# Two more product pairs before the recurrence, their first sums by DMA, and a root taken on GpSimd, in one layer of a streaming encoder

## Time and profile before

| | us |
|---|---|
| median of three runs | 1911.4 (1910.64 to 1913.37) |
| the profiled execution | 1911.61 |
| its span | 1909.8 |
| TensorE busy | 1889.0 (99%) |
| VectorE busy | 1355.4 (71%) |
| ScalarE busy | 859.4 (45%) |
| GpSimd busy | 84.7 (4%) |

### The profile page before, as it was taken

The page is one execution under the profiler, slowest core; times in us unless marked ns, Lnnn a source line. Parts: engine busy times, 40 slices in busy tenths (PEclk is TensorE's granted clock), DMA queues, the critical chain, the costliest instruction groups (busy, mean ns, idle before and its releaser), DMA issues.

```text
span 1909.8 us, 33091 instructions
## 1 busy us (share of the span) xinstructions
PE 1889.0 (99%) x13241; PEld 1864.5 (98%) x13241; DVE 1355.4 (71%) x2078; ACT 859.4 (45%) x1609; POOL 84.7 (4%) x136
## 2 busy tenths in 40 slices
PE   9999999999999999999999999999999999999997
PEld 8999999999999998999999999999999999999997
DVE  7798999899997754773444378976777776736363
ACT  5454444445434455551122355644454444635342
POOL 0010001000111111100000000000000000000000
PEclk9999999999999999999999999999999999999999
DMA  3445555455454754658131322221222223556654
GB/s 134 136 119 129 137 146 139 117 161 169 119 154 117 205 171 124 160 168 331 45 138 45 119 88 102 82 80 68 91 74 75 70 89 108 187 202 208 211 172 153
DMA packets 117031, 255.09 MB, mean 134 GB/s; under 512 B 19980, under 2 KB 59660, under 8 KB 116880
## 3 DMA queue, kind: packets, MB, share of 16 engines
q1 hardware_dynamic: 105936, 223.10, 34.5%
q0 software_dynamic: 10944, 29.89, 8.1%
HBM read 191.44 MB, written 61.51 MB: 132 GB/s over the span
## 4 chain that ended last, share of the span: by engine, by line
PE 90%; DVE 7%; issue 1%; ACT 1%; DMA 1%; SPq 0%; POOL 0%; DVEq 0%; ACTq 0%; POOLq 0%
PE ps L1155 10%; PE ps L1156 10%; PE ps L1157 10%; PE ps L1519 7%; PE ps L1517 7%; PE ps L1518 7%; PE ps L1319 6%; PE ps L1320 6%; PE ps L1321 6%; PE ps L1535 4%; PE ps L1537 4%; PE ps L1536 4%; PE ps L1247 2%; PE ps L1244 1%; DVE cacc L2402 1%
## 5 line engine op out<-in xcount | busy, mean ns | idle before, releaser
L1155 PE MATMUL ps<-rx,fhi 128*128 128x364 f32 (+2 forms) x832 | 280.7, 337 | 0.4 <-ACT qkv L1679 0.2
L1156 PE MATMUL ps<-rx,fhi 128*128 128x364 f32 (+2 forms) x832 | 269.7, 324 | 0.0
L1157 PE MATMUL ps<-rx,flo 128*128 128x364 f32 (+2 forms) x832 | 269.6, 324 | 0.0
L1319 PE MATMUL ps<-rx,ahi 128*128 128x304 f32 (+1 forms) x608 | 175.6, 289 | 0.7 <-DVE v L2522 0.7
L1320 PE MATMUL ps<-rx,ahi 128*128 128x304 f32 (+1 forms) x608 | 175.3, 288 | 0.0
L1535 PE MATMUL ps<-ghi,dhi 128*128 128x384 f32 (+1 forms) x528 | 173.2, 328 | 2.0 <-DVE glo L2872 1.7
L1321 PE MATMUL ps<-rx,alo 128*128 128x304 f32 (+1 forms) x608 | 175.2, 288 | 0.0
L1536 PE MATMUL ps<-glo,dhi 128*128 128x384 f32 (+1 forms) x528 | 172.3, 326 | 0.0
L1537 PE MATMUL ps<-ghi,dlo 128*128 128x384 f32 (+1 forms) x528 | 172.3, 326 | 0.0
L2865 DVE TENSOR_TENSOR dlo<-draw,dhi 128x1408 fp32r<-128x1408 f32 x48 | 77.8, 1624 | 120.3 <-ACT dhi L2095 120.3
L1155 PEld LDWEIGHTS ps<-rx,fhi 128*128 128x128 f32 x832 | 156.8, 188 | 2.3 <-ACT qkv L1679 0.5
(11 more groups left out here) (362 smaller groups left out, 5623.0 us busy)
## 6 DMA issues: line engine op xcount, KB each, us to landing
draw<-wdn SPq DMA_DIRECT2D x48, 704.0 KB, 4.1
uraw<-wts SPq DMA_DIRECT2D x44, 512.0 KB, 4.4
araw<-wts SPq DMA_DIRECT2D x76, 256.0 KB, 3.0
fraw<-wts SPq DMA_DIRECT2D x27, 512.0 KB, 3.9
scr_g<-cva SPq DMA_DIRECT2D x22, 512.0 KB, 2.6
qkv<-scr_qkv SPq DMA_DIRECT2D x18, 544.0 KB, 6.7
alo<-wts POOLq DMA_DIRECT2D x38, 256.0 KB, 5.2
fhi<-wts POOLq DMA_DIRECT2D x19, 512.0 KB, 7.3
```

What stands on the lines that cost most here:

```text
L1155: pe.matmul(b, hi[:, w], src[:, his[k], cols], start=(k == 0), stop=False)
L1156: pe.matmul(b, hi[:, w], src[:, los[k], cols], start=False, stop=False)
L1157: mm = pe.matmul(b, lo[:, w], src[:, his[k], cols], start=False, stop=(k == KB - 1))
L1319: pe.matmul(b, ahi[s][:, c], bhi[:, k, :], start=(fresh and k == 0), stop=False, skip_group_check=True)
```

## The change

1. Head 0's k and v become pairs: 21 pairs in another order, 23 tiles outside. They go to `scr_qkv` and are read back (`load_first_head`); q0 stays a plain tile.
2. s1 of each pair is no longer added by VectorE: SP loads a21 once more into the place of s1, and a DMA from GpSimd's queue adds a22 onto it.
3. The sums of the convolution's blocks 1 to 6 into `csum` are DMAs that add, on GpSimd's queue.
4. The taps are laid out anew: 16 for a pair in place of 15, 330 (not 282) by the end of the pairs; in the last pair 8 of them come after the pieces of product 5.
5. The steps begin 12 slots after the pairs in place of 22, and the gates' work, the norm's and PASS2's slots move up with them.
6. `stat` is made a root by GpSimd, a power of -0.5 for each of the three column pieces; EPS is added in ScalarE's copy. Ln and Exp go.
7. The ring of weight places is shifted (`wslot`), counters are renumbered, some waits are moved (`decs_in` to step 1), and `c_rest` comes later within its slot.

```diff
     return (pair(0) + pair(1) + one("o", 0, 1)
-            + [("gate", 0)] + head(0, "kvq")
+            + [("gate", 0)] + head(0, "q")
...
-           ("v", 3), ("g", 0), ("u", 6), ("q", 3), ("g", 1), ("u", 7), ("g", 2), ("g", 3)]
+           ("v", 3), ("k", 0), ("u", 6), ("v", 0), ("g", 0), ("u", 7), ("q", 3), ("g", 1), ("g", 2), ("g", 3)]
...
+def wslot(n):
+    return n % 3 if n < N_A else (n + 2) % 3
...
-TAPS_AT = [6, 12, 27, 42] + [50 + 15 * i for i in range(NB - 4)] + [282]
+TAPS_AT = [6, 12, 27, 42] + [50 + 16 * i for i in range(NB - 4)] + [330]
...
-    TAPS_SLOT.append(min(TAPS_SLOT[-1] + (0 if len(TAPS_SLOT) in (8, 9) else 5 if len(TAPS_SLOT) < 8 else 4 if len(TAPS_SLOT) < 23 else 3), NOP * KB))
+    TAPS_SLOT.append(min(TAPS_SLOT[-1] + (0 if len(TAPS_SLOT) in (7, 8, 9, 13) else 4 if len(TAPS_SLOT) < 14 else 3), NOP * KB))
...
-STEP_AT = [S_B + 22 + i for i in range(len(STEPS))]
+STEP_AT = [S_B + 12 + i for i in range(len(STEPS))]
...
-PASS2 = {FULL[S_B + at]: k for k, at in enumerate((CONV_END + 10, CONV_END + 12, 51, 53, 55, 59, 60, 61))}
+PASS2 = {FULL[S_B + at]: k for k, at in enumerate((CONV_END + 10, CONV_END + 12, 42, 44, 46, 48, 49, 50))}
...  SP
+            def first_sum(i):
+                sp.dma_start(araw[aslot(i, 5)][:, :], wts[W_B + 2 * i + 1][:, 0:512]).then_inc(a_s1, 16)
...
+            def load_first_head():
+                for x in range(2):
+                    sp.wait_ge(spl_out[x], 16 * V0_STORES[x][NB])
+                sp.wait_ge(v1_out, 16 * V1_STORES[NB])
+                sp.wait_ge(grp_done, b_at(NB - 1, 3, 1))
+                for b in range(4):
+                    sp.dma_start(qkv[0][:, b, :], scr_qkv[0, b]).then_inc(qk_in, 16)
...
                         sp.wait_ge(grp_done, b_at(i, 1, 1))
                         pair_weights(i + 1, 2)
+                        first_sum(i + 1)
...  GpSimd
+            def first_sum(i):
+                pool.wait_ge(a_s1, 16 * (i + 1))
+                pool.dma_start(araw[aslot(i, 5)][:, :], wts[W_B + 2 * i + 1][:, 512:1024], accum_op=ALU.add).then_inc(a_s1_sum, 16)
+
+            def add_sum(j):
+                pool.wait_ge(c_sto[j % 2], 32 * (j // 2 + 1))
...
+                pool.dma_start(csum[:, 0:SEQ], scr_c[j][:, 0:SEQ], accum_op=ALU.add).then_inc(csum_in, 16)
+                pool.dma_start(csum[:, AS0:AW], scr_c[j][:, SEQ:T], accum_op=ALU.add).then_inc(csum_in, 16)
...
             for i in range(NB):
+                first_sum(i)
                 a_rest(i, 2), a_rest(i, 4)
+                for j in range(1, KB - 1):
+                    if STORE_PAIR.get(j) == i - 1:
+                        add_sum(j)
...
+                for c in range(NC):
+                    if s == SLOT["var", 0, c] + 1:
+                        pool.wait_ge(t_free, EVAC_AT[SLOT["var", 0, c]])
+                        pool.tensor_tensor(stat[:, cut(c)], stat[:, cut(c)], eps[:, 1:2].broadcast_to([P, wd(c)]), ALU.pow).then_inc(stat_set, 1)
...  TensorE
-                if s == GATE_END + 13:
+                if s == GATE_END + 8:
                     gate_turn()
...  ScalarE
-                    act.activation(stat[:, cut(c)], b, ACT.Copy, scale=1.0 / D).then_inc(t_free, 1)
+                    act.activation(stat[:, cut(c)], b, ACT.Copy, bias=EPS, scale=1.0 / D).then_inc(t_free, 1)
...
-                if s == GATE_END + 8:
+                if s == GATE_END + 7:
                     act.wait_ge(gate_dve, 12)
...
-                if s == SLOT["var", 0, 2]:
-                    act.wait_ge(t_free, EVAC_AT[s])
-                    act.activation(stat[:, :], stat[:, :], ACT.Ln, bias=eps[:, 0:1]).then_inc(stat_set, 1)
-                if s == SLOT["var", 0, 2] + 1:
-                    act.wait_ge(stat_set, 1)
-                    act.activation(stat[:, :], stat[:, :], ACT.Exp, scale=-0.5).then_inc(stat_set, 1)
...  VectorE
-                dve.tensor_tensor(s1, a21, a22, ALU.add).then_inc(asum, 1)
-                dve.wait_ge(asum, 4 * i + 1)
                 dve.tensor_tensor(a21, a11, a21, ALU.subtract).then_inc(asum, 1)
+                dve.wait_ge(a_s1_sum, 16 * (i + 1))
                 dve.tensor_tensor(s2, s1, a11, ALU.subtract).then_inc(asum, 1)
...
-                        some_taps(t0, t1)
+                        some_taps(t0, t1 if i + 1 < NB else t1 - 8)
...
                     else:
+                        some_taps(t1 - 8, t1)
                         rest(N_A)
...
+                if s == GATE_END + 4:
+                    gate_scans()
                 if s == GATE_END + 5:
-                    gate_scans()
-                if s == GATE_END + 6:
                     gate_exponents()
-                if s == GATE_END + 11:
+                if s == GATE_END + 7:
                     dve.wait_ge(gate_act, 6)
...
-                if s == GATE_END + 17:
+                if s == GATE_END + 9:
                     gate_columns()
...
-                        dve.wait_ge(stat_set, 2)
+                        dve.wait_ge(stat_set, NC)
```

More of the change, by code:

```diff
@@ L1085, in _ @@
         def _(pool):
-            pool.memset(ones[:, :], 1.0).then_inc(begin_set, 1)
-            pool.memset(csum[:, :], 0.0).then_inc(begin_set, 1)
+            pool.memset(ones[:, :], 1.0).then_inc(const_set, 1)
+            pool.memset(csum[:, :], 0.0).then_inc(const_set, 1)
             pool.memset(eps[:, 0:1], EPS).then_inc(const_set, 1)
@@ L1132, in _ @@
                     pool.tensor_tensor(sm[p][:, 6:7], sm[p][:, 4:5], eps[:, 1:2], ALU.pow).then_inc(rs_set, 1)
+                for j, at in STORE_SLOT.items():
+                    if s == at + 2 and j < KB - 1:
+                        add_sum(j)
+                for c in range(NC):
+                    if s == SLOT["var", 0, c] + 1:
+                        pool.wait_ge(t_free, EVAC_AT[SLOT["var", 0, c]])
+                        pool.tensor_tensor(stat[:, cut(c)], stat[:, cut(c)], eps[:, 1:2].broadcast_to([P, wd(c)]), ALU.pow).then_inc(stat_set, 1)
+                if s == S_B + 1:
+                    for j in range(1, KB - 1):
+                        if STORE_PAIR.get(j) == NB - 1:
+                            add_sum(j)
                 if is_last(s) and SLOTS[s][0][0] not in ("mu", "var"):
@@ L1364, in _ @@
                             w = slice(j * P, (j + 1) * P)
-                            pe.matmul(b, fhi[n % 3][:, w], rx[:, j, cols_of(s)], start=(j == 0), stop=False)
-                            mm = pe.matmul(b, fhi[n % 3][:, w], rx[:, KB + j, cols_of(s)], start=False, stop=(j == KB - 1))
+                            pe.matmul(b, fhi[wslot(n)][:, w], rx[:, j, cols_of(s)], start=(j == 0), stop=False)
+                            mm = pe.matmul(b, fhi[wslot(n)][:, w], rx[:, KB + j, cols_of(s)], start=False, stop=(j == KB - 1))
                         mm.then_inc(grp_done, 1)
                     else:
-                        product(b, fhi[n % 3], flo[n % 3], rows, rx, cols_of(s), 3, halfway)
+                        product(b, fhi[wslot(n)], flo[wslot(n)], rows, rx, cols_of(s), 3, halfway)
                     if s == 3:
@@ L1394, in _ @@
                     rows = (lambda k: (c_lo, k + 1)) if n == 0 and c == 0 else None
-                    product(bank(i % 6, 0, wd(c)), fhi[(PB0 + n) % 3], flo[(PB0 + n) % 3], rows, rz, cut(c),
+                    product(bank(i % 6, 0, wd(c)), fhi[wslot(PB0 + n)], flo[wslot(PB0 + n)], rows, rz, cut(c),
                             his=C_HI, los=[k + 1 for k in C_HI])
@@ L1405, in _ @@
                     rows = (lambda k: (zlo, k + 1)) if n == 0 and c == 0 else None
-                    product(bank(i % 6, 0, wd(c)), fhi[(PA0 + n) % 3], flo[(PA0 + n) % 3], rows, rx, cut(c))
+                    product(bank(i % 6, 0, wd(c)), fhi[wslot(PA0 + n)], flo[wslot(PA0 + n)], rows, rx, cut(c))
             def sum_o(p):
@@ L1605, in _ @@
             whole(0)
-            act.wait_ge(const_set, 9)
+            act.wait_ge(const_set, 11)
             x_root(0)
@@ L1712, in a_minus @@
                 s = aslot(i, prod)
-                act.wait_ge(asum, 4 * i + (4 if prod == 2 else 3))
+                act.wait_ge(asum, 3 * i + (3 if prod == 2 else 2))
                 act.wait_ge(w_hi, a_at(i, prod))
@@ L1765, in conv_square @@
             def conv_square(k):
-                act.wait_ge(csum_set, k + 1)
+                act.wait_ge(xc_set, k + 1)
+                if k in (0, KB - 1):
+                    act.wait_ge(csum_set, 1 + (k > 0))
                 act.wait_ge(c_sto[k % 2], 32 * (k // 2 + 1))
@@ L1832, in _ @@
                     act.wait_ge(csq_set, KB)
+                    act.wait_ge(csum_set, 2)
                     act.activation(cacc[:, :], csum[:, :], ACT.Square, scale=KB ** -0.5).then_inc(csq_sq, 1)
@@ L2022, in conv_first @@
                     act.wait_ge(c12_set, given(j, 1))
-                act.wait_ge(const_set, 18)
+                act.wait_ge(const_set, 20)
                 act.wait_ge(ub_halo, 2 * j + t + 1)
@@ L2638, in _ @@
                         .then_inc(nc32, 1)
```

(2 more changed lines are left out.)

124 lines of the change are left out of this document (68 added, 56 removed).

## The result

The changed kernel takes **2066.6 us** (2066.2 to 2068.0), the kernel before 1911.0: a ratio of 1.0817 [1.0803, 1.083], 155.6 us slower. The forecast was 1903, with 1924 as the upper end. One later execution, the profiled one of experiment 7's first kernel, ran at a granted clock of 0.556 from end to end (a span of 3115 us) and is not used.

The account below looks back on a forecast made before the run. TensorE, busy 1889.0 of 1909.8 us, was taken as the bound. From the profiled 1911.6 us, -5.8 - 4.2 - 0.35 + 1.1 + 0.5 = -8.75 gave 1903 us; own range 1901 to 1906, whole range to 1924.

Parts of the forecast that it names:

- 1.4 us, hidden: Root on GpSimd: each of three power pieces takes 1.4 us and hides behind other work, costing 0.
- The waits: Behind the powers: a piece hides 7 us before a step's power, 3 us before PASS2; longer stalls bring 1.8 us of clock.
- The power is slow per column: Rival at the root, chance 0.34: longer power pieces stall the steps and PASS2; 1906 to 1920 at 5 us, 1936 at 15.
- The hold of VectorE for a whole power: At the root: GpSimd's powers exclude VectorE's two-input instructions, 1.2 us in full, counted half as about 0.5 us.
- Two pairs, -5.8: In the pairs: two more pairs replace plain tiles, each saving 2.9 us on TensorE, 5.8 us together.
- s1 level with the fourth block, 0: In the pairs: s1's two DMAs land level with a block awaited anyway, between 0 and 0.5 us per pair, taken as 0.
- The pairs' end, 0: At the last pair: 0.7 us before product 3 go, the gate tile's rest is some 0.7 us late; together 0.
- The gates, +1.1: After the pairs: TensorE waits 1.1 us at `gate_turn` for ScalarE's three Exp; bounds 0 and 4 us.
- The gap that I put at 0.35 us: In the plain slots after the pairs: the wait of ScalarE's square for its block's store should fall, -0.35 us.
- The root, -4.2: At the third `var` piece: without ScalarE's root and table loads the stall goes, 4.2 us, of which 1.8 are clock.
- Steps and second pass, 0: Steps, their taps, PASS2 and head loads keep their distances within two slots; PASS2's last blocks cost 0.

Follow-up runs that it names:

- experiment 7: ScalarE's Ln one slot later, Exp two, second pass's first block one: in experiment 1's kernel (the first) 1908.1 us, in experiment 6's kernel 1905.1 us.
- experiment 3: Separate kernel without the computation, timing GpSimd powers and additions at several widths, alone and beside VectorE: a power of 364 columns took 58.4 us.
- the kernel with one column: Changed kernel with each of the three powers over only its piece's first column, the rest of the root left out: 1905.6 us, 0.9972 of before.
- Experiment 4: Changed kernel with each power shortened to 1, 40 or 92 columns, the rest of the root left out: 1905.6, 1912.4 and 1937.6 us.
- experiment 1: Changed kernel with the three GpSimd powers removed and the root's Ln and Exp back on ScalarE: 1907.2 us, 0.9982 of before.
- experiment 5: experiment 1's kernel with s1 added by VectorE again instead of by two DMAs: 1905.3 us, 0.9969 of before.
- experiment 6: experiment 5's kernel with the gate tile's rest moved ahead of the last pair's eight taps: 1905.0 us, 0.9969 of before.
- experiment 2: Kernel before with only the root changed to three GpSimd powers, its Ln and Exp taken out: 2068.1 us, 1.0823 of before.
- Experiment 8: experiment 5's kernel with two 1.1 us copies of the variance tile onto itself on ScalarE ahead of the Ln: 1908.1 us, 0.9986 of before.

## Why the prediction was wrong

**The step that failed** is the size of the power: "The nearest arithmetic over columns on this engine is the select, 292 ns for 128, at most 2.3 ns a column: a piece of 1.4 us. I take 1.4." It is 160 ns a column, 58.4 us a piece, 70 times the select's price per column (experiment 3). The term "1.4 us, hidden" measures 2066.6 - 1905.6 = 161.0 us against the kernel with one column: three stops of 153.2 us, and 7.8 us more. TensorE runs at 1.2 GHz for 5.1, 4.2 and 2.9 us behind the three stops; half of that, 6.1 us, is my estimate of what the clock takes. The remaining 1.7 are not traced to a place.

Why the choice was wrong can be read from the rows that I had. The select is another instruction. The power was in the trace, at one column, with 552 ns, where a memset of one column has 98:

```profile
L1088 POOL MEMSET eps<- 128x1 f32 x1 | 0.1, 98 | 0.0
```

By taking 1.4 I put nearly all of the 450 ns between them down to set-up. I had written that nothing says so, and nothing did; 145 to 160 of them were the column. The two ends that I wrote down were 0.86 and 200 us. Ends 230 times apart say that the trace does not price the operation, and the range (to 1924) then covered pieces of at most 10 us.

**The waits were right.** "The power is slow per column" stood as the rival, at 0.34: with its two waits, its thresholds (3 us where the second pass waits, 7 us behind a step's power), and at least 1936 us at 15 us a piece. Experiment 4 measured 1937.6 there and a stop only at the third piece for 7.0 us. The near hits are partly luck: the covers are 8 to 10 us and 5, not 7 and 3, and more comes on top of a stop than 1.8 us. What failed was to stop at 15 us: at the upper end of 200 us the same rule gives over 580, at the measured 58.4 it gives (58.4 - 3) + 2 x (58.4 - 7) + 5.4 = 163.6, against 161.0 measured (158.2 of stops for 153.2, and 5.4 behind them for 7.8). The hold of VectorE for a whole power, counted half, was not there: 0, not 0.5. In the changed kernel only VectorE's `zt` at each power's start is longer, 0.84, 0.88 and 0.87 us for 0.41; at the start of pieces of 40 and 92 columns it takes 0.41 to 0.43.

**Two pairs, -5.8.** Right as far as the pairs' length shows. Two pairs more are 336 matmuls at 0.1257 for 288 at 0.1668, and the 21 pairs of experiment 1 run from 78.1 to 522.6, 21.17 us each, beside 21.19 for the 19 of before.

**s1 level with the fourth block, 0.** Mis-sized: 1.9 us in the medians; of TensorE's waits for `v` the traces show 0.3 to 1.8 us (experiment 5). The likely reason: VectorE's slack of 7% is a mean over 350 us, while in experiment 1's kernel the wait for s1 falls in 7 of 21 pairs, up to 3.5 us in one, and the slack of another pair is no help there.

**The pairs' end, 0.** The 0.7 us before product 3 are gone, and the gate tile's rest was 0.9 us late, forecast 0.7. Moving it took that wait away, without a gain that the runs tell (experiment 6).

**The gates, +1.1.** TensorE waits 0.3 us at `gate_turn` (L1255) and 0.9 us at the first scores one slot on (L1275): 1.2 in sum, in another place than forecast for most of it. The columns of the gates were the late part, not the three Exp. The gap that I put at 0.35 us is 0.20 in the trace of before, and it is gone.

**The root, -4.2.** Right for the kernel before: experiment 2 less the 161.0 us of the powers is 1907.1, 3.9 under before (an estimate, if the powers cost the same there). But it is the wrong number to credit to the change. More than half of it came from the place. In the kernel before ScalarE had two full-width copies in the slot ahead of the table load:

```profile
731.34 1.11 ACT L1695 ACTIVATE spl<-spl 128x1088 f32<-128x1088 f32 x1
732.36 1.04 ACT L1580 ACTIVATE flo<-fhi 128x1024 fp32r<-128x1024 f32 x1
```

Experiment 8 puts their length back, and the stop and the half clock come with it. The new distances alone left 1.6 us of the 4.2 (experiment 1 against one column), so the powers had 1.6 to win, not 4.2. That difference of two medians is good to about 1 us: experiment 1's runs (1906.0 to 1909.8) and those of the kernel with one column (1904.9 to 1907.1) overlap, and the stop in experiment 1's trace is 0.8 us.

**Steps and second pass, 0.** With the root gone two stops at L1307, 1.0 us in all, are in the trace of the kernel with one column; apart from the root the kernel before has none there that its waits list. The changed order lets the rest of one block of the second pass (1.28 us of VectorE) fall behind the three operations of the next, ahead of the longer one (0.6 us). That this is its cause was not tried alone, and the shorter one (0.4 us) is not explained.

So with no root and no long power the change is worth 5.6 us (experiment 4, one column). The sum has 9.25 for that, the 8.75 without the 0.5 for the powers' hold. Of the 3.65 between, s1 takes 1.9, the steps 1.0, the gates, the pairs' end and the gap some 0.3 together; the rest is within the spread of the runs.

## What to carry to other kernels

- An operation that the trace shows at one width only has no price per column. Take the difference between its row and the cheapest row of one column as the price of the column until a second width says otherwise: 0.45 us here, within a factor of three of the truth, where the nearest other operation was 70 times off. A move that depends on it is measured first: one small kernel with two widths would have told.
- On an in-order engine the length of a new instruction is paid by what stands behind it. Write the cost as length less cover for each place, and then put the upper end of the length in, not a comfortable one.
- If a power must be on GpSimd, give it few columns and all partitions. These 1088 values stand in all 128 partitions alike; as 128 x 9 they would take 0.4 + 9 x 0.16 = 1.8 us, an estimate from experiment 3 that leaves out bringing them there and back. It wasn't tried.

The best version here keeps the two pairs, with the root on ScalarE and s1 on VectorE (experiments 5 and 6): 1905.0 to 1905.3 us, 0.9969 of before.

## What the runs showed of the hardware

GpSimd's power takes 0.4 us and 160 ns for every column, whether 1, 32 or 128 partitions are used.

VectorE and GpSimd lengthen each other's instructions. Beside GpSimd's additions VectorE's take 1.18 for 0.54 and 0.98 for 0.35 us, those with a single input tile too, and the additions 1.04 for 0.95. Beside a power of 58.7 us only the VectorE instruction at its start is longer, by 0.47 us; powers of 8 columns lengthen none of VectorE's, and take 1.83 for 1.64 us themselves. The Trainium skill ("SBUF — State Buffer", on the shared port pair) has the exclusion for a whole instruction. For the power the trace does not agree. For additions it agrees that both sides are held, but not for their whole durations: two additions and VectorE's two instructions, 2.79 us if one followed the other, take 2.24.

TensorE's granted clock stayed at its upper level, 2.4 GHz, after a stop of 0.8 us (0.998 over that whole kernel) and was at 0.50, 1.2 GHz, after a stop of 3.1 in the profiled execution. Behind stops of 48.9 to 53.3 us it was at 0.50 for 2.9 to 5.1 us.
